# Convolution channels' products in parts of 512, 512 and 32 columns instead of three of 352

## The reference, cut to what matters

```python
u = rmsnorm(x, g_mix)
proj = u @ w_in                       # (rows, 3600), f32
dn_qkv, dn_z, dn_alpha, dn_beta, sb_q, sb_k, sb_v = jnp.split(proj, IN_SPLITS, axis=-1)
c, new_conv = causal_conv(dn_qkv, conv_w, conv_state)   # 4 taps over rows, per channel
c = jax.nn.silu(c)
```

## Time and profile before

| what | value |
|---|---|
| median of 3 runs | 1815.92 us (1814.44 to 1817.2) |
| the profiled execution's own time | 1817.45 us |
| its span, first to last instruction | 1815.7 us |
| TensorE busy | 1686.7 us (93%), 14640 products |
| VectorE, ScalarE, GpSimd busy | 718.1, 454.4, 571.8 us |
| chain of waits, share of TensorE | 80%, line 1987 with 8% of the span |

### The profile page before, as it was taken

How to read it: one execution, slowest core, us unless ns; L and a number is a source line. 1 busy time by engine, 2 the same in 40 slices (tenths; PEclk the granted TensorE clock), 3 DMA queues, 4 the chain that set the end, 5 groups by cost and what they waited for, 6 DMA issues and landing times.

```text
span 1815.7 us, 33086 instructions
## 1 busy us (share of the span) xinstructions
PE 1686.7 (93%) x14640; PEld 1591.8 (88%) x14640; DVE 718.1 (40%) x865; ACT 454.4 (25%) x888; POOL 571.8 (31%) x288
## 2 busy tenths in 40 slices
PE   5889999997999578878999999999999999999998
PEld 5889989995666367778999999999999999999898
DVE  6662033555666477851252121222222221226322
ACT  4322113224666344421131010101010101013111
POOL 5131322322000122234244333434343434342520
PEclk9999999998999688888999999999999999999999
DMA  5112321224002454432311111111111111112121
GB/s 183 46 51 68 104 62 54 100 82 137 1 1 90 117 119 107 93 85 62 86 43 47 47 47 47 47 47 46 44 40 47 47 47 47 47 47 71 47 59 49
DMA packets 199364, 118.58 MB, mean 65 GB/s; under 512 B 65905, under 2 KB 192445, under 8 KB 199228
## 3 DMA queue, kind: packets, MB, share of 16 engines
q1 hardware_dynamic: 187360, 103.54, 20.0%
q10 hardware_dynamic: 11868, 13.02, 2.1%
HBM read 94.69 MB, written 21.84 MB: 64 GB/s over the span
## 4 chain that ended last, share of the span: by engine, by line
PE 80%; DVE 10%; issue 3%; DMA 3%; ACT 2%; SPq 1%; ACTq 0%; POOL 0%; DVEq 0%; POOLq 0%
PE psum L2186 45%; PE psum L1987 8%; PE psum L2481 5%; PE psum L1938 3%; PE psum L1939 3%; PE psum L1940 3%; PE psum L2019 2%; PE psum L2031 2%; PE psum L2049 2%; DVE area L1713 2%; PE psum L2500 1%; DVE area L1538 1%; DVE area L1717 1%; PE psum L2212 1%; DMA area<-x_scratch 1%
## 5 line engine op out<-in xcount | busy, mean ns | idle before, releaser
L2186 PE MATMUL psum<-act_hi,w_round 128*128 128x352 f32 x1920 | 367.9, 324 | 1.6 <-ACT area L1368 1.2
L983 POOL TENSOR_TENSOR w_round<-w_plain,ones 128x1024 fp32r<-128x1024 f32 x80 | 172.6, 2157 | 510.5 <-DMA w_plain<-in_w_up_dram 228.1
L2186 PEld LDWEIGHTS psum<-act_hi,w_round 128*128 128x128 f32 x1920 | 319.9, 189 | 2.7 <-issue 1.8
L2186 PE MATMUL psum<-hid_hi,w_round 128*128 128x352 f32 x1344 | 257.5, 323 | 0.4 <-DVE hid_lo L1884 0.4
L2186 PEld LDWEIGHTS psum<-hid_hi,w_round 128*128 128x128 f32 x1344 | 222.4, 188 | 0.7 <-DVE hid_lo L1884 0.7
L1861 DVE TENSOR_TENSOR area<-psum,area 128x1056 f32<-128x1056 f32 x72 | 90.5, 1257 | 308.1 <-PE psum L2186 308.1
L2186 PE MATMUL psum<-act_lo,w_round 128*128 128x352 f32 x960 | 207.0, 324 | 0.0
L984 POOL TENSOR_TENSOR w_round<-w_plain,w_round 128x1024 fp32r<-128x1024 f32 x80 | 202.4, 2530 | 6.3
L1467 ACT ACTIVATE hid_hi<-area 128x1056 fp32r<-128x1056 f32 x28 | 30.5, 1088 | 589.1 <-DVE area L1877 589.1
L1938 PE MATMUL psum<-w_round,act_hi 128*128 128x256 f32 (+1 forms) x576 | 166.6, 289 | 5.4 <-ACTq L1121 5.4
L1939 PE MATMUL psum<-w_round,act_hi 128*128 128x256 f32 (+1 forms) x576 | 163.6, 284 | 0.0
(11 more groups left out here) (294 smaller groups left out, 2423.4 us busy)
## 6 DMA issues: line engine op xcount, KB each, us to landing
w_plain<-in_w_up_dram SPq DMA_DIRECT2D x32, 512.0 KB, 4.0
w_plain<-in_w_down_dram SPq DMA_DIRECT2D x32, 512.0 KB, 3.4
w_plain<-in_w_in_dram SPq DMA_DIRECT2D x14, 1024.0 KB, 5.5
conv_scratch<-area ACTq DMA_DIRECT2D x12, 512.0 KB, 2.7
area<-in_x_prompt_dram SPq DMA_DIRECT2D x8, 512.0 KB, 3.7
w_plain<-in_cache_k_dram SPq DMA_DIRECT2D x4, 1024.0 KB, 5.5
w_plain<-in_w_out_dram SPq DMA_DIRECT2D x8, 512.0 KB, 5.6
w_plain<-in_x_prompt_dram SPq DMA_DIRECT2D x8, 512.0 KB, 5.0
```

Of the source, the lines that this page charges most:

```text
L983: own.link(pool.tensor_tensor(hi, ring_raw(n), ones[:, 0:1].to_broadcast([P, RB]), ALU.mult))
L2186: last = pe.matmul(bank(bank_set(tile) + c)[:, 0:CH], w(k), a(k)[:, CH * c:CH * (c + 1)], start=(begins and k == ks[0] and w is w_h and a ...
```

## The change

The products of the convolution channels are no longer three parts of 352 columns. The first two take 512 columns of the prompt each, a whole bank of PSUM, and the third the sample's 32 columns. The gate columns keep the thirds. ScalarE's copies follow: 512, 512 and 32 columns, three copies in place of four.

```diff
-                pieces = [(0, 0, CH, 3), (1, 0, CH, 3 + CH), (2, 0, TP - 2 * CH, 3 + 2 * CH),
-                          (2, TP - 2 * CH, CH, TP + 6)]
+                pieces = [(0, 0, 512, 3), (1, 0, 512, 3 + 512), (2, 0, TS, TP + 6)]
                 for b, lo, hi, to in pieces:
                     last = act.activation(x3[:, to:to + hi - lo], bank(3 * odd + b)[:, lo:hi], ACT.Copy)
...
-            def dense(base, lhs_hi, lhs_lo, K=KT, hi=act_hi, lo=act_lo, before=None, rows=P):
+            thirds = [(CH * c, CH * (c + 1)) for c in range(3)]
+            full_banks = [(0, 512), (512, TP), (TP, T)]
+
+            def dense(base, lhs_hi, lhs_lo, K=KT, hi=act_hi, lo=act_lo, before=None, rows=P, parts=thirds):
...
                     for w, a in ((lhs_hi, hi), (lhs_hi, lo), (lhs_lo, hi)):
-                        for c in range(3):
-                            last = pe.matmul(bank(base + c)[0:rows, 0:CH], w(k), a[:, k, CH * c:CH * (c + 1)],
+                        for c, (first, end) in enumerate(parts):
+                            last = pe.matmul(bank(base + c)[0:rows, 0:end - first], w(k), a[:, k, first:end],
...
                     last = dense(3 * (j % 2), lambda k: whi_cols[:, slot, k, P * mm:P * mm + P],
-                                 lambda k: wlo_cols[:, slot, k, P * mm:P * mm + P])
+                                 lambda k: wlo_cols[:, slot, k, P * mm:P * mm + P], parts=full_banks)
```

## The result

The median of the changed kernel is 1840.86 us (four runs, 1837.36 to 1844.99) against 1815.56 us (four runs, 1814.44 to 1817.2): slower, with a ratio of 1.0142, 95% interval 1.0122 to 1.0161, or +25.3 us. The prediction was 1842 (1836 to 1847), slower. The profiled execution took 1844.99 us with a span of 1843.2, 27.5 us more than the span before.

What follows compares the result with a forecast made beforehand. TensorE alone was taken to bound the kernel. The convolution stage's +26.2 us and −0.1 for ScalarE's copies gave +26.1, from a median of 1815.92 to 1842 us; range 1836 to 1847, meant to hold 8 times in 10.

Steps and rivals of the forecast that it cites:

- The two waits named: Convolution stage: POOL's 72.7 us wait for line 1987 and VectorE's first tap's 54.1; idle times grow about as much as the stage.
- The 512-column product: Convolution stage: each was to take 234 ns, bounds 228 to 236, from a line through 256 and 352 columns.
- triple: Three products per weight tile and pass, 288 in the convolution stage: 486.1 ns before, 577 forecast (563 to 584).
- One sign: Sign of being right, in the convolution stage: 512-column products stand 234 ns apart.
- The 32-column product: Convolution stage: 109 ns although its stream is 13, since the next weight load can start only where it starts.
- ScalarE's copies: Convolution stage: four per tile become three, 586 ns for 512 columns; only the last tile's count, −0.1 us.
- The rest at nothing, ±1 us: Engines behind TensorE and later stages: they shift as a whole at no cost, phase effects ±1 us.
- A shorter load: Rival, convolution stage: weight load of 62 ns, as for transposes; +12.6 us, 1828.5 us in all; chance 0.04.
- Two loads for a short product: Rival, convolution stage: the 32-column product costs two loads, another 109 ns per triple; +57.5 us, about 1873.5; chance 0.03.
- Loads two ahead: Rival, convolution stage: loads run two products ahead, the 32-column product costs 13 to 15 ns; −0.9 to −4.6 us; chance 0.05.
- A falling clock: Rival, convolution stage: TensorE's clock falls; at 1.2 GHz throughout a triple is 960 ns or more, +137 us; chance 0.02.
- A hidden change: Rival: the convolution stage's change stays hidden because something else ends the stage; same time; chance 0.01.

## Why the prediction was right

- *The bound.* TensorE alone, in one unbroken piece: it stayed so, and the others' waits grew. The two waits named grew by 17 us, not by the 26 foreseen. By the stretches POOL's whole idle time in the stage did grow by 25.9 us and VectorE's by 19.3, since it was busy for 76.17 us instead of 69.57; why is open.
- *The 512-column product*, 234 ns taken from the line through two shorter ones, 228 to 236 as bounds: (576.0 − 109)/2 = 233.5. That the two rows lie on that line was no reason, since it was drawn through them; its reach to 512 was a guess within close bounds that came out. The 216 of the Trainium skill ("TensorE: Matmul & The Clock Gate", Back-to-back issue gap, which calls it the gap of a single product by itself) was rightly left aside for the row. With its triple of 541 ns the stage would be 155.8 us, an estimate; it took 165.88. One sign was put too simply: the starts of the two 512s of a triple lie 0.32 apart (299.91 and 300.23), since the first one's record holds its wait. The 0.23 stands in the weight loads.
- *The 32-column product*, 109 ns from the f32 products of line 2424: 0.11, and the gate columns and the lengths of the 512s show that it is the load. A row of another line and another type carried the prediction: it had a load of the same size and a product as short.
- *A triple* 577 ns, measured 576.0; *the stage* +26.2, measured +25.87.
- *ScalarE's copies*: 586 ns foreseen for 512 columns, 597 measured; on the path −0.1 foreseen, 1.25 to 1.18 measured.
- *The rest at nothing, ±1 us*: the width was too small. The stretches around the stage moved by −2.9, −1.7, +5.5 and +0.7 us in the profile, so the other stages did not keep their lengths. The first four runs of the changed kernel spread over 7.6 us and the 18 of the kernel before over 13.0, where the forecast had ±1.4. In the first medians this nearly cancelled (+25.3 where the stage alone gives +25.9), in the second it left 1.6 (+27.5). That the time came within 1.2 us of the forecast is in part luck; the stage's 165.88 us are not.
- *Rivals.* A shorter load (62 ns) fell: no step under 0.11 behind a short part in any of these stages. Two loads for a short product fell: 864 records. Loads two ahead fell: one step of 0.11 per triple remains in every kernel with a short part, also where two loads, 0.22 us, would fit under a 512. A falling clock in this stage: 1.00 in the changed kernel. A hidden change: the stage's growth is in the span.

What stays open is why the streams are longer than their columns at 2.4 GHz; no run was made for it.

## What to carry to other kernels

Cut a moving operand into equal parts rather than into full banks and a remainder: a part must stream for at least as long as the next product's weight load, and here the break-even lies between 192 and 272 columns for a load of 128. Where a remainder can't be avoided, put it in front of a narrow load, or share it out as 512 + 272 + 272 does, at no cost. Look for this in the starts of the weight loads, or in the length of the product behind the short one (0.48 against 0.40 us): TensorE's busy share and idle time don't show it.

## What was not expected of the hardware

- The time that a stream loses is not fixed per product but grows with its columns: 272 columns take 124 ns (113.3 at 2.4 GHz), 352 take 162 (146.7), 512 take 233.5 (213.3), all at a granted clock of 1.00. That is 0.456 to 0.460 ns a column, so a whole bank saves next to nothing even where no load sticks out (1.2 us of 140 with 512, 272 and 272).
- In the kernel with the gate columns in full banks the clock fell near the start of the convolution stage. The stretches there:

```profile
266.00:279.60 13.60, 12.37 (x82) 5.71 (x80) 3.51 (x1) 1.51 (x4) 8.29 (x2) 1.00 0.28 85
279.60:286.00 6.40, 6.40 (x26) 5.40 (x26) 0.47 (x2) 6.25 (x15) 0.00 (x0) 0.73 0.01 3
286.00:289.00 3.00, 3.00 (x17) 2.53 (x16) 0.61 (x5) 0.62 (x2) 0.00 (x0) 1.00 0.00 0
```

  A mean of 0.73 over 6.4 us, between the levels of 1.2 and 2.4 GHz, and 1.00 again behind it. Ahead of it TensorE made the gate columns, waited for ScalarE's copies and made nine short transposes, as in every kernel here, and in the changed kernel's profile the clock stays at 1.00 there. The stage is 1.5 us longer than in the changed kernel, which a clock of 0.73 over 6.4 us accounts for (27% of it are 1.7). It was seen in one run of one kernel, and why it fell there is open.
